# Three attention sweeps on one core: weights turned two steps behind their score, and one run of projection matmuls per step

## The chip, the cores and the metric

The kernel runs on 1 core of one Trainium2 chip. The metric is the device time of one execution in microseconds (us); the median of three runs stands below. Engines are named as the profile names them: PE (TensorE matmuls), PEld (its weight loads), DVE (VectorE), ACT (ScalarE), POOL (GpSimd), SP (SyncE, which issues DMAs).

## What is computed

Three layers on 512 tokens of width 1024, in fp32. Cut to the parts that matter here:

```
def mla_mixer(c_q, c_kv, k_r, pos, ...):                   # layer 1, 12 heads of 64 + 32 rotary
    q  = (rms_norm(c_q, q_norm) @ w_q_up).reshape(B, S, MLA_HEADS, MLA_QK)
    kv = (rms_norm(c_kv, kv_norm) @ w_kv_up).reshape(B, S, MLA_HEADS, MLA_NOPE + MLA_V)
    return causal_block_attention(qf, kf, v, MLA_QK ** -0.5)
def fox_mixer(q, k, v, f_logit, b_f):                      # layer 2, 12 heads of 64
    return causal_block_attention(qh, kh, vh, FOX_DIM ** -0.5, log_f_cum)
def memory_attention(q, k, v):                             # in layers 1 and 2, 4 heads, 256 memory rows
    s = einsum('bshd,bmhd->bhsm', q, k) * MEM_DIM ** -0.5
    return einsum('bhsm,bmhd->bshd', softmax(s), v)
def stick_breaking(q, k, v):                               # layer 3, 16 heads of 64
    log_fail = where(mask, log_sigmoid(-logits), 0)
    between  = cumsum(log_fail, reverse) - log_fail
    w        = where(mask, exp(log_sigmoid(logits) + between), 0);  out = w @ v
```

Every layer is h + rms_norm((attention * silu(gate)) @ w_out) with projections of the normed h ahead of it; the third also has a scan branch.

## The kernel before

The engines' programs are written out by hand, in order, with semaphores between them. A projection in fp32 is three fp32r matmuls for each block: the activations' high part with the weights' high part, high with low, low with high. A weight piece of 1024 columns (512 KB) comes by SP's DMA, ACT writes its high part (`high_part`, L510), POOL the rest (`rest`, L515).

Each attention is a *sweep* over pairs of heads, four steps a pair. A step s is one block of 128 queries for both heads of a pair; its two items are 2s and 2s + 1. The blocks of a causal pair come in the order 3, 0, 2, 1, with 512, 128, 384 and 256 keys. Both layer 1 and layer 2 have 32 steps: two memory pairs (steps 0 to 7, 256 keys) and six causal pairs (8 to 31). Layer 3 has eight causal pairs, also 32 steps. The work of a step:

- PE `score(s)`: L836 (L1910 in layer 3), in layer 1 also L840 for the rotary part, and the mask by a bf16 matmul at L843 (L1913), into banks 2 to 5.
- DVE `lowest` (L933, in layer 2 L929), ACT `exp` (L896), DVE `share` (L939, L942): the weights, in one of four buffers. In layer 3 ACT takes two sigmoids per item (L1984, L1988) and DVE a scan (L2036) and a product (L2042).
- PE `turn_w(i)` (L854, L1925) transposes an item's weights into bank 6 or 7; ACT `collect_w(i)` (L907, L1998) copies them out. `turn_w(i)` waits until item i - 2 is copied out.
- once a pair, PE `values(p)` (L868, L1937) into bank 1, and DVE `weigh` (L950) multiplies by the gate.
- between these, PE projects the next pairs' queries and keys into bank 0: `turn_in(n)` issues the next n matmuls (L1182, L1371, L1894). ACT's `collect(q)` (L1250, L1395, L1971) copies a finished projection q out of bank 0, and `split_ahead_act` then makes the high part of piece q + 2. The first matmul of projection q + 1 waits for that copy. When none is left, `turn_in` issues a filler (`keep_busy`, L668).

In layer 1 two more things stand in the first eight steps: eight units of the values' projection (`v_unit`, L1199; two of them ahead of the sweep, one in each of the steps of `V_STEPS`), whose results ACT or DVE copies out (L1271, L1286), and four transposes of rotary parts (`turn_rope`, L1168) that DVE copies out (L1290). The first causal score waits for all of them.

PE's steps are cut by `counts(s)`, two numbers, matmuls before and after the transposes. The loop before is

```
for s in range(steps + 2):
    score(s)
    before, after = counts(s)
    turn_in(before)
    if beside: beside(s)
    if s % 4 == 1: values(s // 4 - 1)
    turn_w(2 * s - 2); turn_w(2 * s - 1)
    turn_in(after)
```

Each step therefore turns the weights of step s - 1. ACT's loop is exp of step s, `between(s)`, collect_w of step s - 1, `after(s)`; DVE's is lowest, share, weigh, `after(s)`.

Of the kernel before, what the change touches and what calls it, by code (L numbers as in the profile page):

```python
# [30 lines left out]
MB = T // P  # L31
# [188 lines left out]
def build(nc, i, out):  # L220
    ctx = ExitStack()
    with ctx:
# [597 lines left out]
        def sweep_pe(pe, A, turn_in, counts, beside=None):  # L820
# [37 lines left out]
            def values(p):  # L858
                if not 0 <= p < len(A.pairs):
                    return  # L860
                X = A.pairs[p]
                pe.wait_ge(*A.weights_in(8 * p + 8))
                if p:
# [20 lines left out]
        def sweep_act(act, A, between, after):  # L884
# [26 lines left out]
            for s in range(steps + 1):  # L911
# [3 lines left out]
                collect_w(2 * s - 2)  # L915
                collect_w(2 * s - 1)
                after(s)

        def sweep_dve(dve, A, after):
# [33 lines left out]
            for s in range(steps):  # L953
# [4 lines left out]
                if s % 4 == 1:  # L958
                    weigh(s // 4 - 1)
# [186 lines left out]
        V_STEPS = (0, 1, 2, 3, 4, 6)  # L1146
# [7 lines left out]
        def mla_pe(pe):  # L1154
# [32 lines left out]
            def v_unit(u):  # L1187
# [6 lines left out]
                if u == 7:  # L1194
                    pe.wait_ge(*attA.gated(1))
# [30 lines left out]
            def counts(s):  # L1226
                if s < 4:
                    return ((5, 0), (4, 0), (3, 0), (3, 0))[s]
                if s < 4 * MP:
                    return 1, 0  # L1230
# [8 lines left out]
            sweep_pe(pe, attA, turn_in, counts, beside)  # L1239

        def mla_act(act):
# [11 lines left out]
            def after(s):  # L1253
# [7 lines left out]
                if s > last:  # L1261
# [12 lines left out]
            sweep_act(act, attA, between, after)  # L1274
# [3 lines left out]
        def mla_dve(dve):  # L1278
# [17 lines left out]
            sweep_dve(dve, attA, after)  # L1296
# [53 lines left out]
        def fox_pe(pe):  # L1350
# [26 lines left out]
            def counts(s):  # L1377
                if s < 4 * MP:
                    return 6, 0
                if s < 4 * (MP + B_H // 2 - 1):  # L1380
                    return ((8, 6), (8, 2), (10, 6), (8, 0))[s % 4]
                if s < 4 * (MP + B_H // 2):
                    return 3, 3
                return (0, 4) if s % 4 == 0 else (4, 0)
            sweep_pe(pe, attB, turn_in, counts)

        def fox_act(act):
# [10 lines left out]
            def piece(s):  # L1398
                if s < 4 * MP:
                    return s // 4  # L1400
                return 2 * (s // 4 - MP) + 2 + (s % 4 == 3)

            def between(s):
                if s % 4 == 3 and s < 4 * (MP + B_H // 2 - 1):
                    collect(piece(s))

            def after(s):
                if s % 4 == 1 and 4 * MP <= s < 4 * (MP + B_H // 2 - 1):
                    collect(piece(s))
                    split_ahead_act(act, S, 0, piece(s))  # L1410
                if s % 4 == 3 and s < 4 * (MP + B_H // 2 - 1):
                    split_ahead_act(act, S, 0, piece(s))
                if s == 4 * (MP + B_H // 2 - 1):
                    act.wait_ge(C["product"].sem, S.done_after(0, S.n - 1, 0))
                if s > 4 * (MP + B_H // 2 - 1):
                    gated_high(act, attB, s - 4 * (MP + B_H // 2 - 1) - 1)
            sweep_act(act, attB, between, after)
# [3 lines left out]
        def fox_dve(dve):  # L1421
# [5 lines left out]
            sweep_dve(dve, attB, after)  # L1427
# [451 lines left out]
        def stick_pe(pe):  # L1879
# [62 lines left out]
            turn_in(48 + 4)  # L1942
            for s in range(STEPS + 1):
                score(s)
                before, after = ((8, 6), (8, 2), (10, 6), (8, 0))[s % 4]
                before -= 4 * (s == 0)
                if s >= STEPS - 4:
                    before, after = ((6, 6), (6, 6), (6, 6), (6, 0), (6, 0))[s - STEPS + 4]
                turn_in(before)
                if s % 4 == 1:  # L1950
                    values(s // 4 - 1)
                turn_w(2 * s - 2)
                turn_w(2 * s - 1)
                turn_in(after)
# [3 lines left out]
        def stick_act(act):  # L1958
# [47 lines left out]
            for s in range(STEPS + 1):  # L2006
# [3 lines left out]
                if s % 4 == 3 and s < STEPS - 1 or s == STEPS:  # L2010
                    collect(2 * PAIRS + 1 if s == STEPS else 2 * p + 3)
                collect_w(2 * s - 2)
                collect_w(2 * s - 1)
                if s % 4 == 1:
                    collect(2 * p + 2)
                    split(2 * p + 2)
                if s % 4 == 3 and s < STEPS - 1 or s == STEPS:
                    split(2 * PAIRS + 1 if s == STEPS else 2 * p + 3)

        def stick_dve(dve):  # L2020
# [11 lines left out]
            for i in range(2 * STEPS):  # L2032
# [11 lines left out]
                if i % 8 == 2:  # L2044
# [360 lines left out]
```

## Time and profile before

| what | value |
|---|---|
| device time, median of 3 runs | 1221.72 us (1221.5 to 1224.92) |
| the profiled execution's own time | 1220.76 us |
| its span, first to last instruction | 1219.0 us |
| PE busy | 1195.6 us (98%) |
| DVE, ACT, POOL busy | 535.0, 592.5, 429.7 us |
| PE clock granted | 0.999 of full speed |

The span is the time that the trace shows; 1.8 us of the execution's own time lie around it. PE's matmuls are pipelined: a matmul's duration in the trace (0.39 us for 512 columns) is longer than the distance to the next one's start (0.23 us), so what a sequence costs is read from starts, not from durations.

### The profile page before, as it was taken

How to read it: one execution, taken by the hardware profiler on the slowest of the kernel's cores; microseconds unless marked ns; L12 is line 12 of the kernel's file. 1: busy time of each engine (PE TensorE's matmuls, PEld its weight loads, DVE VectorE, ACT ScalarE, POOL GpSimd, SP SyncE). 2: the span in 40 equal slices, each digit the busy share in tenths (PEclk: the TensorE clock that was granted, in tenths of full speed). 3: DMA queues.
4: the chain of work that ended last, by engine and by line, in shares of the span. 5: the costliest groups of instructions: out<-in, count | busy, mean ns of one | idle time of the engine just before them, and what ended most of it. 6: DMA issues, size and time to landing. Idle time of an engine off the chain costs nothing. (4 is left out here: it accounts for less than half of the span.)

```text
span 1219.0 us, 16491 instructions
## 1 busy us (share of the span) xinstructions
PE 1195.6 (98%) x6261; PEld 931.1 (76%) x6261; DVE 535.0 (44%) x978; ACT 592.5 (49%) x1246; POOL 429.7 (35%) x259
## 2 busy tenths in 40 slices
PE   8999999999999999999999999999999999999998
PEld 8988855578988666678888987787666667878886
DVE  4311465643310555452566745601767660033333
ACT  6444655645442655554644654534655552333142
POOL 6534711204344222215344333343322223434451
PEclk9999999999999999999999999999999999999999
DMA  8433211103335999713232321233111113323231
GB/s 310 122 104 67 64 22 44 55 23 95 89 107 81 89 66 73 109 52 89 75 99 56 119 63 59 83 90 104 53 52 52 53 53 91 99 88 103 89 102 69
DMA packets 111407, 100.99 MB, mean 83 GB/s; under 512 B 21141, under 2 KB 98273, under 8 KB 111329
## 3 DMA queue, kind: packets, MB, share of 16 engines
q1 hardware_dynamic: 108784, 95.35, 33.5%
q0 software_dynamic: 864, 3.15, 0.7%
q10 hardware_dynamic: 1680, 1.44, 0.4%
q8 instruction: 50, 0.82, 0.3%
q14 instruction: 29, 0.23, 0.1%
HBM read 94.68 MB, written 2.10 MB: 79 GB/s over the span
## 5 line engine op out<-in xcount | busy, mean ns | idle before, releaser
L515 POOL TENSOR_TENSOR w_lo<-w_raw,w_hi 128x1024 fp32r<-128x1024 f32 (+6 forms) x161 | 362.5, 2252 | 718.6 <-ACT w_hi L510 718.6
L510 ACT ACTIVATE w_hi<-w_raw 128x1024 fp32r<-128x1024 f32 (+6 forms) x161 | 159.9, 994 | 236.1 <-PE bank L570 212.3
L570 PE MATMUL bank<-acts_hi,w_hi 128*128 128x512 f32 (+1 forms) x576 | 224.7, 390 | 3.2 <-DVE acts_lo L2057 1.6
L570 PE MATMUL bank<-acts_lo,w_hi 128*128 128x512 f32 (+1 forms) x576 | 222.9, 387 | 0.0
L570 PE MATMUL bank<-acts_hi,w_lo 128*128 128x512 f32 (+1 forms) x576 | 222.8, 387 | 0.0
L570 PEld LDWEIGHTS bank<-acts_hi,w_hi 128*128 128x128 f32 x576 | 108.3, 188 | 27.9 <-issue 3.8
L570 PEld LDWEIGHTS bank<-acts_lo,w_hi 128*128 128x128 f32 x576 | 108.2, 188 | 22.0
L570 PEld LDWEIGHTS bank<-acts_hi,w_lo 128*128 128x128 f32 x576 | 108.3, 188 | 21.2
L2036 DVE TENSOR_TENSOR_SCAN arena_end<-arena 128x512 f32<-128x512 f32 (+3 forms) x64 | 80.8, 1262 | 63.2 <-ACT arena L1984 63.2
L570 PE MATMUL bank<-w_hi,acts_hi 128*128 128x512 f32 (+4 forms) x248 | 90.0, 363 | 1.6 <-DVE arena L950 1.6
L570 PE MATMUL bank<-w_hi,acts_lo 128*128 128x512 f32 (+4 forms) x248 | 89.4, 361 | 0.0
L570 PE MATMUL bank<-w_lo,acts_hi 128*128 128x512 f32 (+4 forms) x248 | 89.2, 360 | 0.0
L570 PE MATMUL bank<-w_more,acts_hi 128*128 128x512 f32 (+3 forms) x296 | 75.4, 341 | 0.0
L942 DVE TENSOR_SCALAR arena<-arena,stat 128x256 f32<-128x256 f32 (+3 forms) x128 | 65.7, 513 | 4.5
L933 DVE TENSOR_REDUCE stat<-bank 128x1 f32<-128x256 f32 (+3 forms) x80 | 33.4, 458 | 74.3 <-PE bank L836 47.7
L907 ACT ACTIVATE arena<-bank 128x256 f32<-128x256 f32 (+3 forms) x128 | 47.0, 422 | 36.3 <-PE bank L854 36.2
L896 ACT ACTIVATE arena<-bank,stat 128x256 f32<-128x256 f32 (+3 forms) x80 | 39.8, 504 | 39.3 <-DVE stat L933 39.3
L515 POOL TENSOR_TENSOR w_more<-w_raw,w_more 128x1024 fp32r<-128x1024 f32 (+4 forms) x21 | 43.5, 2085 | 43.5 <-ACT w_more L510 43.4
L1894 PE MATMUL bank<-acts_hi,w_hi 128*128 128x512 f32 x144 | 58.6, 407 | 0.0
L1894 PE MATMUL bank<-acts_hi,w_lo 128*128 128x512 f32 x144 | 58.5, 406 | 0.0
L1894 PE MATMUL bank<-acts_lo,w_hi 128*128 128x512 f32 x144 | 57.7, 401 | 0.0
L570 PEld LDWEIGHTS bank<-w_more,acts_hi 128*128 128x128 f32 x296 | 51.6, 189 | 3.8
(293 smaller groups left out, 2142.3 us busy)
## 6 DMA issues: line engine op xcount, KB each, us to landing
w_raw<-in_w_in SPq DMA_DIRECT2D x64, 512.0 KB, 3.6
w_raw<-in_w_out SPq DMA_DIRECT2D x24, 512.0 KB, 3.5
w_raw<-in_w_in_b SPq DMA_DIRECT2D x22, 512.0 KB, 5.3
w_raw<-in_w_in_a SPq DMA_DIRECT2D x10, 512.0 KB, 3.9
w_raw<-in_w_mem_kv SPq DMA_DIRECT2D x8, 512.0 KB, 8.5
w_raw<-in_w_sb_proj SPq DMA_DIRECT2D x8, 512.0 KB, 3.4
w_raw<-in_w_ssd_proj SPq DMA_DIRECT2D x8, 512.0 KB, 3.5
arena_shared<-junk SPq DMA_DIRECT2D x11, 256.0 KB, 20.7
```

The source lines that it names most:

```text
L510: nc.scalar.activation(w_at(p)[0][:, 0:size], w_raw[p % RAW][:, 0:size], ACT.Copy).then_inc(w_high.sem, 1)
L515: nc.gpsimd.tensor_tensor(lo[:, 0:size], w_raw[p % RAW][:, 0:size], hi[:, 0:size].bitcast(F32), ALU.subtract).then_inc(w_rest.sem, 1)
L570: mm = nc.tensor.matmul(bank_of(S, s, g)[0:lhs.shape[1], 0:rhs.shape[1]], lhs, rhs, start=j + kk + t == 0, stop=j == len(S.pieces) - 1 and ...
L896: nc.scalar.activation(w2[i % 4][:, 0:n], src[:, 0:n], ACT.Exp, bias=stat[:, i % 8:i % 8 + 1], scale=-1.0 if X.less else 1.0, accum_out=st ...
L907: nc.scalar.activation(wT2[e][:, 0:blocks, b * P:(b + 1) * P], bank[6 + i % 2][:, 0:blocks * P].rearrange("p (c t) -> p c t", c=blocks), A ...
L933: nc.vector.tensor_reduce(stat[:, i % 8:i % 8 + 1], bank[2 + i % 4][:, 0:n], AX.X, ALU.max, negate=True).then_inc(A.lowest.sem, 1)
L942: nc.vector.tensor_scalar(w2[i % 4][:, 0:n], w2[i % 4][:, 0:n], stat[:, 16 + i % 8:17 + i % 8], None, ALU.mult).then_inc(A.weights.sem, 1)
L1894: mm = nc.tensor.matmul(qk_bank(q)[:, :], w[:, kk * P:(kk + 1) * P], acts[:, kk, :], start=x == 0, stop=x == 23)
L2036: nc.vector.tensor_tensor_scan(left[i % 2][:, T - n:T][:, ::-1], x, x, 1.0, ALU.mult, ALU.bypass).then_inc(sem["scan"], 1)
```

## The change

- In all three sweeps the transposes stand two steps behind: step s turns items 2s - 4 and 2s - 3, and ACT collects them in its step s. The values of a pair come at s % 4 = 2, ahead of the transposes, and `weigh` follows.
- The two runs of projection matmuls of a step are one, at its end. What a step takes is a new table, such that a projection ends with step 0 or 2 of a pair, and ACT collects it there, after `collect_w`.
- The sweep of layers 1 and 2 takes three closing steps where it took two, with 26 fillers in all where there were 32.
- In layer 1 `v_unit` stands ahead of the projections of its step, its last unit in step 5 (was 6), and `values(0)` waits for the copy of it.

```diff
-            for s in range(steps + 2):
+            for s in range(steps + 3) if lag == 2 else ():
+                score(s)
+                if s % 4 == 2:
+                    values(s // 4 - 1)
+                turn_w(2 * s - 4)
+                turn_w(2 * s - 3)
+                if beside:
+                    beside(s)
+                turn_in(counts(s))
...
-                collect_w(2 * s - 2)
-                collect_w(2 * s - 1)
+                collect_w(2 * s - 2 * lag)
+                collect_w(2 * s - 2 * lag + 1)
...
-                if s % 4 == 1:
+                if s % 4 == lag:
                     weigh(s // 4 - 1)
...
-        V_STEPS = (0, 1, 2, 3, 4, 6)
+        V_STEPS = (0, 1, 2, 3, 4, 5)
...
-                    return ((5, 4), (0, 3), (3, 0), (0, 0))[s % 4]
+                    return (QN, 0, KN, 0)[s % 4]
                 if s < 4 * (MP + A_H // 2):
-                    return 3, 3
-                return (0, 4) if s % 4 == 0 else (4, 0)
+                    return 6 * (s % 4 < 3)
+                return 4 * (s % 4 < 2)
...
-                if s < 4 * (MP + B_H // 2 - 1):
-                    return ((8, 6), (8, 2), (10, 6), (8, 0))[s % 4]
+                    return (8, 8, 8, 8, 8, 8, 5, 5)[s]
+                if s < 4 * (MP + B_H // 2 - 1) - 1:
+                    return (14, 10, 14, 10)[s % 4]
...
-            turn_in(48 + 4)
-            for s in range(STEPS + 1):
+            turn_in(48 + 10)
+            for s in range(STEPS + 2):
                 score(s)
...
+                if s > STEPS - 4:
+                    turn_in(6 * (s <= STEPS))
+                else:
+                    turn_in((14, 10, 14, 10)[s % 4])
```

QN is 9 and KN is 6. `last` in ACT's new `after(s)` of layer 2 is step 28; `ended_at` names the steps after which a projection is collected: 2, 5, 8, 10, 12 and so on to 26.

**PE, layer 2, a causal pair.** From the projection matmuls that end step 0 to those of step 1; `waits` names semaphores. Before:

```order
L1371 MATMUL bank<-acts_hi,w_lo 128x512
L836 MATMUL bank<-arena 128x128 [waits lowest]
L836 MATMUL bank<-arena 128x128
L843 MATMUL bank<-later_keys,ident_b 128x128 x2
L1371 MATMUL bank<-acts_lo,w_hi 128x512
```

and now, where the last matmul of the run is also the last of a projection:

```order
L836 MATMUL bank<-arena 128x256
L843 MATMUL bank<-later_keys,ident_b 128x128 x2
L854 MATMUL bank<-ident,arena 128x128 [waits weights_in,weights] x2
L1380 MATMUL bank<-acts_hi,w_hi 128x512 [waits qk_in,w_rest]
L1380 MATMUL bank<-acts_hi,w_lo 128x512
```

The mask's matmul was followed by a projection run; now the transposes follow it and the run comes after them, so the run ahead of the transposes is gone. The second piece is a step 3 with two transposes, then the first matmul of a projection with its wait for the copy out of bank 0.

**PE, layer 1, steps 1 and 2.** `v_unit` is L1199 before, L1208 after; the projection run L1182 before, L1193 after. Before:

```order
L836 MATMUL bank<-arena_end 128x256 x2
L1182 MATMUL bank<-acts_lo,w_hi 128x512
L1182 MATMUL bank<-acts_hi,w_hi 128x512
L1182 MATMUL bank<-acts_hi,w_lo 128x512
L1182 MATMUL bank<-acts_lo,w_hi 128x512
L1199 MATMUL bank<-w_more,acts_hi 128x384 [waits evac]
```

and now:

```order
L836 MATMUL bank<-arena_end 128x256 x2
L1208 MATMUL bank<-w_more,acts_hi 128x384 [waits evac]
L1208 MATMUL bank<-w_more,acts_hi 128x384
L1208 MATMUL bank<-w_more,acts_lo 128x384
L1208 MATMUL bank<-w_more,acts_hi 128x384 x2
L1208 MATMUL bank<-w_more,acts_lo 128x384
L1193 MATMUL bank<-acts_lo,w_hi 128x512
```

The unit's wait for the copy of the unit before it (`evac`) moved ahead of the projection run.

**PE, layer 2, from the last score (step 31) to the last values.** Before:

```order
L836 MATMUL bank<-arena 128x256
L843 MATMUL bank<-later_keys,ident_b 128x128 x2
L668 MATMUL bank<-tri_le,ident 128x128 x3
L854 MATMUL bank<-ident,arena 128x128 [waits weights_in,weights]
L854 MATMUL bank<-ident,arena 128x128 x2
L854 MATMUL bank<-ident,arena 128x128 [waits weights_in,weights]
L854 MATMUL bank<-ident,arena 128x128 x2
L668 MATMUL bank<-tri_le,ident 128x128 x3
```

and now:

```order
L843 MATMUL bank<-later_keys,ident_b 128x128 x2
L854 MATMUL bank<-ident,arena 128x128 [waits weights_in,weights] x3
L854 MATMUL bank<-ident,arena 128x128 x2
L854 MATMUL bank<-ident,arena 128x128 [waits weights_in,weights]
L854 MATMUL bank<-ident,arena 128x128 x2
L668 MATMUL bank<-tri_le,ident 128x128 x4
L854 MATMUL bank<-ident,arena 128x128 [waits weights_in,weights]
L854 MATMUL bank<-ident,arena 128x128
```

Step 31 has no filler now, and step 32's transposes stand right behind step 31's.

## Rows read from the trace of the kernel before

**Rows 1.** The page: span, and PE's busy time.

```profile
span 1219.0 us, 16491 instructions
PE 1195.6 (98%) x6261; PEld 931.1 (76%) x6261; DVE 535.0 (44%) x978; ACT 592.5 (49%) x1246; POOL 429.7 (35%) x259
```

**Rows 2.** Windows: us, busy PE, PEld, DVE, ACT, POOL (instructions), clock, DMA.

```profile
139.05:165.17 26.12, 23.30 (x136) 16.52 (x136) 19.85 (x57) 16.77 (x54) 16.81 (x28) 1.00 0.15 33
165.17:253.88 88.71, 88.59 (x543) 50.89 (x543) 50.45 (x142) 50.68 (x156) 11.60 (x10) 1.00 0.15 44
400.44:423.58 23.14, 22.89 (x116) 14.68 (x116) 15.71 (x49) 16.03 (x50) 4.75 (x2) 1.00 0.93 72
423.58:514.11 90.53, 90.40 (x488) 60.02 (x488) 46.94 (x149) 47.63 (x127) 21.66 (x9) 1.00 0.94 94
514.11:533.81 19.70, 19.67 (x130) 14.00 (x129) 11.53 (x38) 12.32 (x33) 7.10 (x11) 1.00 0.25 81
533.81:543.13 9.32, 7.86 (x62) 5.75 (x61) 4.59 (x16) 6.25 (x19) 0.00 (x0) 1.00 0.01 2
843.44:1000.57 157.13, 156.00 (x846) 104.74 (x845) 113.16 (x135) 91.36 (x223) 38.42 (x16) 1.00 0.20 56
```

**Rows 3.** Waits of PE, layers 2 and 3: us in total, times, longest.

```profile
PE bank L854 <- ACT arena L907: 0.7, 1, 0.7
PE bank L1925 <- DVE arena L2042: 0.8, 2, 0.4
```

**Rows 4.** Timeline of PE, layer 2, end of a pair: start us, us, instruction.

```profile
479.01 0.40 PE L1371 MATMUL bank<-acts_hi,w_hi 128*128 128x512 f32 x1
479.34 0.70 PE L836 MATMUL bank<-arena 64*128 64x256 f32 x4
479.97 0.29 PE L843 MATMUL bank<-later_keys,ident_b 128*128 128x128 bf16 x2
480.07 0.47 PE L1371 MATMUL bank<-acts_hi,w_lo 128*128 128x512 f32 x1
480.38 0.39 PE L1371 MATMUL bank<-acts_lo,w_hi 128*128 128x512 f32 x1
480.61 0.40 PE L1371 MATMUL bank<-acts_hi,w_hi 128*128 128x512 f32 x1
...
481.77 0.39 PE L1371 MATMUL bank<-acts_lo,w_hi 128*128 128x512 f32 x1
482.00 0.82 PE L854 MATMUL bank<-ident,arena 128*128 128x128 f32 x6
482.85 1.13 PE L836 MATMUL bank<-arena 64*128 64x512 f32 x4
```

**Rows 5.** Timeline of PE, layer 1: a mask with the transposes right behind it.

```profile
178.87 0.29 PE L843 MATMUL bank<-later_keys,ident_b 128*128 128x128 bf16 x2
179.00 0.83 PE L854 MATMUL bank<-ident,arena 128*128 128x128 f32 x6
```

**Rows 6.** Timeline of ACT, layer 2: a projection is copied out of bank 0.

```profile
482.20 0.60 ACT L1395 ACTIVATE arena<-bank 128x512 f32<-128x512 f32 x1 [0.34 <-PE bank L1371]
```

**Rows 7.** Timeline of DVE and PE, layer 1, memory pairs.

```profile
143.07 0.54 DVE L1286 COPY hn<-bank 128x384 f32<-128x384 f32 x1
...
156.26 1.94 PE L868 MATMUL bank<-arena,arena_end 128*64 128x512 f32 x8
...
158.24 0.69 DVE L950 TENSOR_TENSOR arena<-bank,arena 128x512 f32<-128x512 f32 x1 [0.39 <-PE bank L868]
...
164.39 0.68 DVE L1290 TENSOR_SCALAR arena<-bank 128x512 f32<-128x512 f32 x1
```

**Rows 8.** Timeline of ACT, POOL and DVE, layer 2, steps 27 and 28.

```profile
523.25 1.07 ACT L510 ACTIVATE w_hi<-w_raw 128x1024 fp32r<-128x1024 f32 x1
...
524.39 2.37 POOL L515 TENSOR_TENSOR w_lo<-w_raw,w_hi 128x1024 fp32r<-128x1024 f32 x1 [6.08 <-ACT w_hi L510]
...
525.83 1.21 DVE L942 TENSOR_SCALAR arena<-arena,stat 128x512 f32<-128x512 f32 x1
...
527.15 0.49 DVE L942 TENSOR_SCALAR arena<-arena,stat 128x512 f32<-128x512 f32 x1
```

**Rows 9.** Timeline of ACT and PE, layer 2, behind the last score (533.81).

```profile
536.35 0.49 ACT L896 ACTIVATE arena<-arena,stat 128x256 f32<-128x256 f32 x1
...
537.45 0.80 PE L854 MATMUL bank<-ident,arena 128*128 128x128 f32 x4 [0.67 <-ACT arena L907]
...
539.96 2.37 PE L868 MATMUL bank<-arena 128*64 128x512 f32 x16
```

More of the change, by code:

```diff
@@ L862, in values @@
                 pe.wait_ge(*A.weights_in(8 * p + 8))
+                if bank_free and p == 0:
+                    pe.wait_ge(*bank_free)
                 if p:
@@ L870, in values @@
                 mm.then_inc(A.valued.sem, 1)
-            for s in range(steps + 2):
+            for s in range(steps + 3) if lag == 2 else ():
[7 more added lines that the diff above has]
+                turn_in(counts(s))
+            for s in range(steps + 2) if lag == 1 else ():
                 score(s)
@@ L882, in sweep_pe, with sweep_act @@
                 turn_in(after)
-        def sweep_act(act, A, between, after):
+        def sweep_act(act, A, between, after, lag=1):
             steps = len(A.steps)
@@ L909, in collect_w @@
                                      ACT.Copy).then_inc(A.weights_in.sem, 1)
-            for s in range(steps + 1):
+            for s in range(steps + lag):
                 exp(2 * s)
@@ L914, in sweep_act, with sweep_dve @@
                 between(s)
-                collect_w(2 * s - 2)
-                collect_w(2 * s - 1)
+                collect_w(2 * s - 2 * lag)
+                collect_w(2 * s - 2 * lag + 1)
                 after(s)
-        def sweep_dve(dve, A, after):
+        def sweep_dve(dve, A, after, lag=1):
             steps = len(A.steps)
@@ L1238, in mla_pe @@
             pe.wait_ge(*pA_qr.evac(MB))
-            sweep_pe(pe, attA, turn_in, counts, beside)
+            sweep_pe(pe, attA, turn_in, counts, beside, lag=2, bank_free=pA_v.evac(2 * MB))
         def mla_act(act):
@@ L1260, in after @@
                     split_ahead_act(act, S, 0, q)
-                if s > last:
+                if last < s <= last + 4:
                     gated_high(act, attA, s - last - 1)
@@ L1273, in mla_act @@
             keep_v(1)
-            sweep_act(act, attA, between, after)
+            sweep_act(act, attA, between, after, lag=2)
             for c in range(4, len(attA.pairs)):
@@ L1295, in after @@
                     gated_low(dve, attA, s - last - 2)
-            sweep_dve(dve, attA, after)
+            sweep_dve(dve, attA, after, lag=2)
             for c in range(2, len(attA.pairs)):
@@ L1396, in collect @@
                                      scale=(HD ** -0.5, 1.0)[q % 2]).then_inc(qk_in.sem, 1)
[L1398 to L1405, printed above, removed]
-            def after(s):
[L1408 to L1413, printed above, removed]
+            ended_at = {2: 0, 5: 1}
+            ended_at.update((4 * MP + 2 * n, 2 + n) for n in range(S.n - 2))
+            last = 4 * (MP + B_H // 2 - 1)
+            def after(s):
+                if s in ended_at:
+                    collect(ended_at[s])
+                    split_ahead_act(act, S, 0, ended_at[s])
+                if s == last:
                     act.wait_ge(C["product"].sem, S.done_after(0, S.n - 1, 0))
-                if s > 4 * (MP + B_H // 2 - 1):
-                    gated_high(act, attB, s - 4 * (MP + B_H // 2 - 1) - 1)
-            sweep_act(act, attB, between, after)
+                if last < s <= last + 4:
+                    gated_high(act, attB, s - last - 1)
+            sweep_act(act, attB, lambda s: None, after, lag=2)
             for c in range(4, len(attB.pairs)):
@@ L1426, in after @@
                     gated_low(dve, attB, s - 4 * (MP + B_H // 2 - 1) - 2)
-            sweep_dve(dve, attB, after)
+            sweep_dve(dve, attB, after, lag=2)
             for c in range(2, len(attB.pairs)):
@@ L1940, in values @@
                 mm.then_inc(sem["s_out"], 1)
-            turn_in(48 + 4)
-            for s in range(STEPS + 1):
+            turn_in(48 + 10)
+            for s in range(STEPS + 2):
                 score(s)
[L1945 to L1950, printed above, removed]
-                    values(s // 4 - 1)
-                turn_w(2 * s - 2)
-                turn_w(2 * s - 1)
-                turn_in(after)
+                if s % 4 == 2:
+                    values(s // 4 - 1)
+                turn_w(2 * s - 4)
+                turn_w(2 * s - 3)
+                if s > STEPS - 4:
+                    turn_in(6 * (s <= STEPS))
+                else:
+                    turn_in((14, 10, 14, 10)[s % 4])
             pe.wait_ge(sem["sig"], 4 * STEPS)
@@ L2005, in stick_act @@
             split(1)
-            for s in range(STEPS + 1):
+            for s in range(STEPS + 2):
                 p = s // 4
@@ L2009, in stick_act @@
                 chances(2 * s + 1)
[L2010 to L2018, printed above, removed]
+                collect_w(2 * s - 4)
+                collect_w(2 * s - 3)
+                if s % 2 == 0 and s < STEPS - 2 or s == STEPS:
+                    q = 2 * PAIRS + 1 if s == STEPS else 2 * p + 2 + s % 4 // 2
+                    collect(q)
+                    split(q)
         def stick_dve(dve):
```

17 lines of the change are left out of this document (7 added, 10 removed).

## The prediction

> **What bounds the kernel now.** I read the page first: PE is busy for 1195.6 of 1219.0 us [rows 1], so only what PE issues, or waits for, can change the time. Next the windows over the three sweeps, cut at the score of step 0, of step 8, of the last pair and of step 31 [rows 2]. The causal steps of layers 1 and 2 leave PE almost nothing idle: 90.40 busy of 90.53 us in layer 2's, 88.59 of 88.71 in layer 1's. The gaps are at the ends: the memory steps of layer 1 (23.30 of 26.12) and the 9.32 us behind layer 2's last score (7.86). Then PE's waits: 0.7 us for one `collect_w` at the end of layer 2, 0.8 in two places for the stick-breaking weights, once at the start and once at the end of layer 3 [rows 3]. Last the timeline of one pair, where the distance between starts shows what an order costs [rows 4, 5].
>
> **What the merged runs save.** In the middle of a projection run the next matmul starts 0.23 us after the last (480.38 to 480.61). The first of a run takes 0.31 (480.07 to 480.38) [rows 4]. Ahead of it the mask's two matmuls take 0.10 (479.97 to 480.07); with transposes behind them they take 0.13 (178.87 to 179.00) [rows 4, 5]. So each run that started behind a mask cost 0.08 - 0.03 = 0.05 us more than it will when it joins the run that starts behind the transposes. The other borders (run to score, transposes to run, values) stay as many as they were. Layer 1 loses two such run starts a pair, x5 = 0.5 us. Layer 2 loses four a pair (0.05 each, 0.19 with roundings), x5 = 0.95, and six in the memory steps, where no mask stands ahead and I take 0.1 each with the two borders of `values(0)`: 0.8. Layer 3: 7 pairs x 0.19, and a little at the ends, 1.4.
>
> A second gain is a wait. At the end of a pair the projection's last matmul starts at 481.77 [rows 4]; ACT's copy of it runs from 482.20 to 482.80 [rows 6] and the next pair's score starts at 482.85 [rows 4]. The transposes ahead of it (six from 482.00, 0.11 apart) would have let it start at 482.75. The keys are now ready one step earlier, so 0.1 us goes, in 5 pairs of layer 2 and 7 of layer 3, and 0.2 more at layer 2's step 8: 0.7 and 0.7. Layer 3's two waits of 0.4 for the weights (0.8 [rows 3], some 1.1 counted between starts) go too, as the weights have a whole step more.
>
> **What the change costs.** *Layer 1's start, +0.7.* `v_unit(3)` waits until DVE has copied unit 2 out, which ends at 143.61 [rows 7]. Before, four projection matmuls covered this; now it follows the score of step 1, whose 0.63 us end at some 142.8 by my count, and PE stands for 1.0 us. That alone would be made good by step 5. But the first causal score waits for DVE's last rotary copy (ends 165.07 [rows 7], score 165.17 [rows 2]), and that chain gets longer: in step 6 the two exps need the transposes that now stand behind `values(0)` (1.94 us [rows 7]), and DVE does `weigh` (0.69) and a rotary copy (0.68) [rows 7] after them, ahead of the maxima of step 7. Laying the steps out one by one with these durations I get 165.9 for the score.
>
> *Layers 1 and 2, last pair.* `turn_w(i)` needs item i - 2 copied out, and ACT copies that only after the exps of the step before. With a run of ten matmuls in step 3 of a pair this is hidden. Step 27 has no run left. In layer 2 ACT then goes from the projection's copy (1.1 us after its last matmul's start) to the high part of the next piece (1.07 [rows 8]), to two exps and to the copy: the transposes of step 28 stand some 0.65 us.
>
> Worse, POOL starts its 2.37 us on that piece right behind the high part. In the trace a `share` that starts meanwhile (525.83) takes 1.21 us instead of 0.49 and ends just after POOL does [rows 8]. After the change the shares of step 27, two instead of one, fall into POOL's time; DVE reaches the maxima of step 28 at 2.2 us later than the score allows, and step 29's transposes, which need a copy behind the exps of step 28, stand 1.75 us. So layer 2 pays 2.4. In layer 1 the score is longer (L840), which covers the first and most of the second: 0.3.
>
> *Behind the last score, +0.25 each in layers 1 and 2.* Before, the last transposes start at 537.45, 3.64 us behind the score at 533.81, and the values at 539.96 [rows 9]. Now step 32's transposes stand first: they need the copy of step 29's weights, which ACT does after the last exp (starts 536.35 [rows 9]), so about 3.4 us behind the score; then 6 transposes (0.65), four fillers (0.9), 4 transposes (0.45), four fillers (0.9): values at 6.4 instead of 6.15. That six fillers fewer are issued therefore gives nothing back.
>
> *Smaller.* The lag leaves two transposes fewer ahead of layer 2's last score (-0.2, they stand in the tail) and two more in layer 1's causal window (+0.2). Layer 3: the fourth projection starts at step 1 with no transposes ahead and waits 0.3 for the copy of the third; `turn_w(60)` 0.25. The DMAs are the same and so is their order; SP is ahead by four pieces and POOL's piece is needed 3 us or more after it ends: nothing.
>
> **Sum.** Layer 1: +0.7 - 0.5 + 0.2 + 0.3 + 0.25 = +0.9. Layer 2: -0.95 - 0.8 - 0.7 - 0.2 + 2.4 + 0.25 = 0.0. Layer 3: -1.4 - 0.7 - 1.1 + 0.55 = -2.7. Together -1.8 us: the profiled execution's 1220.76 becomes 1219.0. The median stands 0.96 above that execution, so I predict 1219.9. The unknown terms are layer 1's start (0 to 1.2) and layer 2's last pair (0 to 3, by whether the shares meet POOL's instruction and for how long).
>
> **A rule that speaks against the gain.** The trace shows 0.31 for the first matmul of a run, although the mask, the transposes and the projections all use the whole array (128*128 [rows 4]). The Trainium skill (TensorEngine Tiling (Array Packing), "Key Properties") says that changing the tiling mode drains TensorE. By that rule alone only scores (64*128) and values (128*64) would cost a change, the change has just as many of these, and the 3.65 us of the run starts would not be there: the sum would be -1.8 + 3.65 = +1.85, 1223.6. I go by the row.
>
> **The rivals.**
> 1. *All of it is hidden* (0.18). ACT and DVE keep up in the last pairs and layer 1's start is as long as before. For it: they are busy less than half the time [rows 1]. Against: the ends of the sweeps are where PE waits today. Without the waits that I add (0.7, 0.3, 2.4, 0.55, 0.5) it is -6.2 us: 1215.5; without the meeting with POOL alone (1.75 + 0.3) -3.9: 1217.8.
> 2. *Bank 0 comes free too late* (0.07), slower. A projection now ends a step, and the next starts behind one score and two or four transposes: 0.33 to the score, 0.63 for it, 0.13 for the mask, 0.11 for the transposes [rows 4, 5], 1.2 us after the last matmul's start. The copy ends 1.03 after it [rows 6], up to 1.1 where ACT has another wait ahead of it, and PE sees it 0.05 later. So 0.05 us is what is left, at some 25 places of layers 2 and 3. If ACT is still at `collect_w` (moved ahead of the copy) or at a delayed exp when the projection ends, each place costs the delay: 0.3 us each would be +7.5, 1225.7 after everything else. It decides from about 0.2 us each. Against: by the durations ACT is free 1 us or more ahead.
> 3. *Run starts cost the same wherever they stand* (0.05), so that 3.65 us of the gain is not there: the cost sits in the change of the kind of matmul and not in a run's start, 1223.6, within 0.3%.
>
> **How the numbers follow.** A measurement of this kernel can tell about 0.3%, 3.7 us, from no change. My forecast has 0.70: 1219.9, with bounds of its own of 1217.8 to 1222.5 by the two unknown terms; 0.02 of it lies below -3.7. Faster by over 0.3%: that and rival 1, 0.20. Slower: rival 2 less the 0.01 where its delay is small, 0.06. The same: the rest with rival 3, 0.74. The range leaves out the best end of rival 1 and most of rival 2: 1216.6 to 1223.2.
>
> **What would show it.** In the changed profile a causal pair of layer 2 should take 19.6 us from score to score (19.9 before), one of layer 1 14.9 (15.0), one of layer 3 19.6. The first matmul of a run should still take 0.31. Layer 1's step 8 score should start 26.8 us behind its first (26.1 before), with PE idle about 1 us ahead of `v_unit(3)`. Layer 2's steps 28 and 29 should show waits of PE at the transposes, for `collect_w`, of 0.6 and 1.7 us, and a `share` of step 27 of some 1.5 to 2 us. The wait ahead of step 32's transposes should be 1.5 us or more. No wait for the stick-breaking product should be left. I am wrong if the pairs' time does not fall, if waits for `collect(q)` stand ahead of the first matmuls of projections, or if the last pairs show none.

## The result, and the profile after

The changed kernel takes 1224.67 us (median of 21 executions, 1223.28 to 1226.30), the kernel before 1221.69 (21 executions); the ratio is 1.0017, its 95% interval [1.0011, 1.0024], all of it above 1. I predicted 1219.9, a range of 1216.6 to 1223.2, and most likely no difference that can be told. The difference is indeed under 0.3%, but it is on the other side, 3.0 us slower instead of 1.8 faster, and above the range. The profiled execution is the longest of the 21, 1226.30 us, 5.5 above the one of before. The traces explain these 5.5; for the median, 1.6 below that execution, they are a guide.

The page of the changed kernel, its span, PE's busy time and the line of PE's granted clock. In the clock's line each digit is a slice of 30.6 us; the 8 is the slice from 153 us:

```profile
span 1224.6 us, 16443 instructions
PE 1192.8 (97%) x6237; PEld 931.0 (76%) x6237; DVE 541.6 (44%) x978; ACT 590.5 (48%) x1246; POOL 431.3 (35%) x259
PEclk9999989999999999999999999999999999999999
```

PE is busy 2.8 us less than in [rows 1] and the span is 5.6 longer: it waits more. The windows of the same places as in [rows 2] (us, busy PE, PEld, DVE, ACT, POOL, clock, DMA):

```profile
139.74:166.49 26.75, 22.85 (x133) 15.76 (x132) 20.04 (x57) 16.14 (x52) 16.76 (x28) 1.00 0.15 31
166.49:174.55 8.06, 8.06 (x23) 4.16 (x23) 2.57 (x6) 2.00 (x6) 0.00 (x0) 0.58 0.00 0
406.57:430.79 24.22, 24.22 (x122) 15.51 (x122) 15.06 (x47) 15.99 (x49) 7.15 (x3) 1.00 0.93 81
430.79:516.82 86.03, 85.92 (x469) 58.55 (x468) 50.06 (x147) 44.42 (x122) 19.05 (x8) 1.00 0.95 84
516.82:541.55 24.73, 20.71 (x141) 13.79 (x140) 14.01 (x45) 13.29 (x39) 6.92 (x11) 1.00 0.31 103
541.55:552.68 11.13, 8.16 (x51) 6.19 (x51) 4.56 (x14) 6.88 (x19) 0.00 (x0) 0.85 0.01 1
854.39:1006.12 151.73, 151.59 (x840) 103.61 (x839) 115.21 (x135) 89.43 (x222) 39.62 (x16) 1.00 0.20 56
```

The second row is layer 1's step 8, 8.06 us at a mean granted clock of 0.58, where every window of [rows 2] has 1.00. The one before last is layer 2's tail at 0.85, 11.13 us instead of 9.32. Layer 1's tail reads the same:

```profile
258.08:269.26 11.18, 8.79 (x55) 6.48 (x54) 4.52 (x12) 6.73 (x19) 0.00 (x0) 0.85 0.00 0
```

against 9.27 before. So in three stretches of 6.8, 3.4 and 3.4 us, starting at 166.6, 262.2 and 545.5, the granted clock is at its lower level of 1.2 GHz. (Both traces have one more in their last 4 us, where PE runs nothing.) How PE comes to the first, and below it to the second, in its timeline:

```profile
162.44 0.68 PE L854 MATMUL bank<-ident,arena 128*128 128x128 f32 x4 [0.25 <-ACT arena L918]
163.87 0.66 PE L1179 MATMUL bank<-ident,arena 128*128 128x128 f32 x4 [0.74 <-DVE arena L1299]
166.49 1.98 PE L836 MATMUL bank<-arena 64*128 64x512 f32 x4 [1.96 <-issue]
168.39 2.08 PE L840 MATMUL bank<-arena 32*128 32x512 f32 x4
...
261.46 0.84 PE L854 MATMUL bank<-ident,arena 128*128 128x128 f32 x6 [1.60 <-ACT arena L918]
```

PE had been idle for 0.25, 0.74 and 1.96 us within 4.3 us; then the score takes 1.90 us to the start of its rotary part (1.06 at full clock, in e2 below). The kernel before also stands there, 0.17 us and then 1.79 in one piece, and its score runs at full clock, 1.06 us to the rotary part:

```profile
165.17 1.13 PE L836 MATMUL bank<-arena 64*128 64x512 f32 x4 [1.79 <-issue]
```

So what is new ahead of step 8 is above all more waits in a row; the long one grew by 0.17. Layer 2's tail:

```profile
544.88 0.92 PE L854 MATMUL bank<-ident,arena 128*128 128x128 f32 x6 [2.18 <-ACT arena L918]
545.60 1.92 PE L668 MATMUL bank<-tri_le,ident 128*128 128x128 f32 x8
547.30 1.06 PE L854 MATMUL bank<-ident,arena 128*128 128x128 f32 x4
```

Four fillers (eight matmuls in the trace) take 1.70 us from start to start, against 0.9 at full clock (e1 below). The third new thing is in layer 2's step 26. PE, and ACT in step 24:

```profile
517.67 0.29 PE L843 MATMUL bank<-later_keys,ident_b 128*128 128x128 bf16 x2
519.86 2.37 PE L870 MATMUL bank<-arena 128*64 128x512 f32 x16 [1.90 <-ACT arena L918]
```

```profile
513.54 0.60 ACT L1404 ACTIVATE arena<-bank 128x512 f32<-128x512 f32 x1 [0.83 <-PE bank L1380]
517.45 1.06 ACT L510 ACTIVATE w_hi<-w_raw 128x1024 fp32r<-128x1024 f32 x1 [3.30 <-DMA w_raw<-in_w_out]
```

ACT stood 3.30 us for the DMA of a piece of the output weights, with the exps of step 25 (from 518.41) and the copies that the values need queued behind it.

Where the 5.5 us between the two profiled executions come from, by place (score starts; the low clock's share is the place's time less the same place at full clock in the runs below):

| place | predicted | measured |
|---|---|---|
| ahead of layer 1's first score (nothing changed there) | 0 | +0.7 |
| layer 1, step 0 to 8 | +0.7 | 26.75 - 26.12 = +0.6 |
| layer 1, step 8 to 31 | 0.0 | +2.9, of it low clock +3.2 |
| layer 1, tail | +0.25 | 11.18 - 9.27 = +1.9, of it low clock +1.65 |
| layer 2, step 0 to 31 | -0.25 | 134.98 - 133.37 = +1.6, of it DMA wait 1.9 |
| layer 2, tail | +0.25 | 11.13 - 9.32 = +1.8, of it low clock +1.6 |
| layer 3, from its first projection matmul | -2.7 | -4.0 |

### The profile page after: what moved, and what is told of

Read it like the earlier page. It is cut to its first block, busy times and chain, and to the rows that moved or that the text cites. A ratio compares the mean times of both kernels' runs of the same rounds, so it can differ in the third digit from the quotient of the medians.

```text
span 1224.6 us, 16443 instructions
## 1 busy us (share of the span) xinstructions
PE 1192.8 (97%) x6237; PEld 931.0 (76%) x6237; DVE 541.6 (44%) x978; ACT 590.5 (48%) x1246; POOL 431.3 (35%) x259
## 4 chain that ended last, share of the span: by engine, by line
PE 87%; DMA 5%; ACT 3%; DVE 2%; issue 1%; POOL 1%; SPq 0%; ACTq 0%; DVEq 0%
PE bank L570 47%; PE bank L1896 8%; PE bank L1589 6%; PE bank L1380 3%; PE bank L836 3%; PE bank L854 3%; PE bank L870 3%; PE bank L1912 2%; DMA w_raw<-in_w_out 2%; DMA w_raw<-in_w_in_b 2%; PE bank L1193 2%; PE bank L1927 2%; PE bank L1939 2%; DMA w_raw<-in_w_mem_kv 1%; PE bank L840 1%
## 5 line engine op out<-in xcount | busy, mean ns | idle before, releaser
L2033 DVE TENSOR_TENSOR_SCAN arena_end<-arena 128x512 f32<-128x512 f32 (+3 forms) x64 | 83.9, 1310 | 60.3 <-ACT arena L1984 60.3
L953 DVE TENSOR_SCALAR arena<-arena,stat 128x256 f32<-128x256 f32 (+3 forms) x128 | 71.2, 557 | 4.5
L854 PE MATMUL bank<-ident,arena 128*128 128x128 f32 x304 | 47.2, 284 | 6.6 <-ACT arena L918 6.6
```

The lines of the kernel that those rows point to most:

```text
L854: mm = nc.tensor.transpose(bank[6 + i % 2][:, c * P:(c + 1) * P], w2[i % 4][:, c * P:(c + 1) * P], ident[:, :])
L953: nc.vector.tensor_scalar(w2[i % 4][:, 0:n], w2[i % 4][:, 0:n], stat[:, 16 + i % 8:17 + i % 8], None, ALU.mult).then_inc(A.weights.sem, 1)
L2033: nc.vector.tensor_tensor_scan(left[i % 2][:, T - n:T][:, ::-1], x, x, 1.0, ALU.mult, ALU.bypass).then_inc(sem["scan"], 1)
```

## The experiments

The theory after reading the traces: the change shortens the pairs as predicted; it lost because new idle time of PE lets the clock fall to 1.2 GHz in layer 1's step 8 and in two tails, and because the earlier high part waits for its DMA. The rivals: the places are long for other reasons and the clock is beside the point; run starts cost nothing; ACT is overloaded. The kernel before, measured again beside each group of runs, had medians of 1221.64 to 1221.69. The runs are called e1 to e12.

**Fillers in the tails (e1).** In both layers' `counts`:

```diff
-                    return 6 * (s % 4 < 3)
+                    return (6, 6, 6, 8)[s % 4]
```

> The changed kernel with 8 filler matmuls in step 31 of layers 1 and 2, where it has none; they stand in the time in which PE waits for step 32's transposes (1.60 and 2.18 us in the changed kernel's trace). Theory clock: PE's idle time there lets the granted clock fall to the 1.2 GHz level, and the transposes and fillers behind it cost double; from the last score to the last values should be 6.3 us in both layers instead of 8.0, the clock of these stretches 1.0, and the kernel about 3 us faster than the changed one: 1221.5. Rival chain: the last values are late by ACT's and DVE's chain of the last weights, whatever PE does meanwhile; the stretch stays at 8.0 us and the time at 1224.7.

1221.48 us, ratio to before 0.9993 [0.9983, 1.0003]. Both tails at full clock; layer 1's, score to values:

```profile
256.40 0.70 PE L836 MATMUL bank<-arena 64*128 64x256 f32 x4
...
258.02 1.95 PE L668 MATMUL bank<-tri_le,ident 128*128 128x128 f32 x16
259.81 0.83 PE L854 MATMUL bank<-ident,arena 128*128 128x128 f32 x6
260.47 1.06 PE L668 MATMUL bank<-tri_le,ident 128*128 128x128 f32 x8
261.36 0.60 PE L854 MATMUL bank<-ident,arena 128*128 128x128 f32 x4
262.79 2.37 PE L870 MATMUL bank<-arena,arena_shared 128*64 128x512 f32 x16
```

The values start 6.39 us behind the score, where the changed kernel takes 8.02. The edit adds 24 fillers: 8 in each tail and, as `counts` of layer 2 uses this line from step 27 on, 8 in layer 2's step 27, where they take the place of waits (steps 27 to 31 take 15.15 us with and without them). This work that nobody reads makes the kernel 3.2 us faster: the clock theory, and not a chain of ACT and DVE. Layer 1's step 8 is at 1.2 GHz in this trace too, for 3.4 us instead of 6.8 (6.42 us instead of 8.06), so some of the profiled executions' difference is how long a low stretch lasts.

**Fillers in layer 1's step 7 (e2).**

```diff
+                if s == 4 * MP - 1:
+                    pe.wait_ge(*attA.gated(1))
+                    keep_busy(pe, 3, 1)
...
                         turn_rope(x - QKN)
+                        if x == QKN + RG:
+                            keep_busy(pe, 8, 1)
```

> The changed kernel with fillers in layer 1's step 7: 3 ahead of the last rotary transposes (wait of 1.0 us there) and 8 behind them (2.0 us). Theory clock: the step 8 score, its rotary part and the projection run behind it took 3.15 us more than before only since the clock was at 1.2 GHz after the idle time; step 8 to 9 should take 4.9 us instead of 8.06, and the kernel 1221.5, 3.1 less than the changed one. The chain of DVE that delays the score of step 8 by 0.6 us stays. Rival contention: the 8.06 us come from something else in that place (the DMAs, or a wait for bank 0) and stay: 1224.7.

1219.26 us, 0.9971 [0.9960, 0.9983]: 5.4 less than the changed kernel, more than the 3.1 expected. Step 8 of it:

```profile
164.64 1.95 PE L668 MATMUL bank<-tri_le,ident 128*128 128x128 f32 x16
166.65 1.13 PE L836 MATMUL bank<-arena 64*128 64x512 f32 x4
167.71 1.13 PE L840 MATMUL bank<-arena 32*128 32x512 f32 x4
```

The window of step 8 is 4.87 us:

```profile
166.65:171.52 4.87, 4.87 (x23) 2.68 (x24) 2.11 (x6) 1.70 (x6) 0.00 (x0) 1.00 0.00 0
```

The score comes as late as before the edit, 26.75 us behind the first: that delay costs 0.6 and is another matter (e12); the other 3.2 were the clock. The surprise is the rest: both tails are at full clock too, although they have the same waits as in the changed kernel (1.6 and 2.2 us). The idle time makes the fall possible, it does not bring it each time.

**Layer 1 as before (e3).** `mla_pe`, `mla_act`, `mla_dve` and `V_STEPS` of the kernel before, the rest as changed.

> Layer 1's sweep as in the kernel before, layers 2 and 3 as changed. Theory clock plus the terms read from the two traces: layer 1 costs +0.64 (start) +2.88 (step 8 at half clock less the merged runs) +1.91 (tail) = 5.4 us in the profiled executions; without it the kernel should be at about 1219.5, 2 below the kernel before, and its trace should show only one stretch at 1.2 GHz, behind layer 2's last score. If the low clock in the profiled execution is rare in the other executions, the gain is the 0.9 us of start and tail alone: 1223.8.

1219.53 us, 0.9980 [0.9968, 0.9991], as the clock theory said and far from the 1223.8 of its rival. One low stretch, in layer 2's tail:

```profile
536.02:547.20 11.18, 8.21 (x52) 6.14 (x51) 4.64 (x14) 6.94 (x19) 0.00 (x0) 0.85 0.01 1
```

**Layer 3 alone (e4).** `stick_pe`, `stick_act` and `stick_dve` as changed, the rest as before.

> Only layer 3's sweep as changed, layers 1 and 2 as before. By the prediction's terms -2.7 us (1219.0); by the two traces -4.05 us (1217.6): the window from its first projection matmul to the end of the sweep. No stretch of the trace should be at 1.2 GHz behind the first layer's start. If the run starts had cost nothing (rival 3 of the prediction), -1.3: 1220.4.

1217.56 us, 0.9964 [0.9954, 0.9975]: -4.1, the traces' term and not the prediction's. Here the third part of the change beats the kernel before by itself.

**Two runs of projection matmuls a step, lag kept (e8)** (on the kernel of the last experiment):

```diff
                 score(s)
+                ahead = (6, 0, 6, 0)[s % 4] if 0 < s <= STEPS - 4 else 0
+                turn_in(ahead)
...
-                    turn_in((14, 10, 14, 10)[s % 4])
+                    turn_in((14, 10, 14, 10)[s % 4] - ahead)
```

> As e4_l3_alone (layer 3 as changed, the others as before), but in steps 0 and 2 of a pair of layer 3 six of the 14 projection matmuls stand ahead of the transposes, behind the mask: two more run starts a pair, the lag and everything else as in e4. Theory of the prediction: 0.05 us each, a pair 19.6 instead of 19.50, the kernel 0.7 to 0.8 slower than e4: 1218.3. Rival 3 (run starts cost the same wherever they stand, the gain comes from the lag alone): pairs at 19.50, 1217.6.

1218.41 us, 0.9968 [0.9957, 0.9979], 0.85 above e4. A causal pair of e4, then of this kernel:

```profile
862.05:881.54 19.49, 19.49 (x109) 13.30 (x108) 14.14 (x17) 11.30 (x28) 4.78 (x3) 1.00 0.19 55
```

```profile
864.20:883.87 19.67, 19.67 (x110) 13.20 (x109) 14.11 (x17) 11.31 (x28) 4.76 (x3) 1.00 0.20 53
```

A run start behind the mask costs 0.09 us (0.18 for two), more than the 0.05 predicted. From the first score of layer 3 to the last the two traces differ by 1.25 us, the medians by 0.85. Rival 3 of the prediction falls. This trace also has a low stretch of 3.4 us in layer 1's step 8, where its program is that of the kernel before:

```profile
166.47:172.95 6.48, 6.48 (x24) 3.77 (x24) 2.57 (x6) 2.12 (x6) 0.00 (x0) 0.74 0.00 0
168.40:171.80 3.40, 3.40 (x12) 2.48 (x11) 2.31 (x6) 1.45 (x4) 0.00 (x0) 0.50 0.00 0
```

**The high part behind layer 2's projection 10 one step later (e5).** It is the high part of the first piece of the output weights (`in_w_out` in the rows above), made when projection 10 is copied out.

```diff
                     collect(ended_at[s])
-                    split_ahead_act(act, S, 0, ended_at[s])
+                    if s < last - 4:
+                        split_ahead_act(act, S, 0, ended_at[s])
+                if s == last - 3:
+                    split_ahead_act(act, S, 0, S.n - 2)
+                if s == last - 2:
+                    split_ahead_act(act, S, 0, S.n - 1)
```

> The changed kernel, but in layer 2 ACT makes the high part of the last but one piece at the end of step 25 instead of step 24, where in the changed kernel's trace it waits 3.30 us for that piece's DMA with the exps of step 25 queued behind it. Theory DMA: PE's 1.90 us ahead of the values in step 26 is this wait passed on; it should be gone, step 26 to 27 take 7.6 us instead of 9.57 and the kernel 2 us less, 1222.7. Rival: values in step 26 wait for ACT's copies because ACT has too much in its steps 24 and 25; the wait stays at 1 us or more and the time at 1224. The waits of steps 28 and 29 stay (0.5 and about 1.5).

1222.24 us, 0.9999 [0.9990, 1.0009], 2.4 less than the changed kernel. PE's values in step 26, 0.22 us behind the mask's last start (517.48), and ACT in step 25:

```profile
517.70 2.38 PE L870 MATMUL bank<-arena 128*64 128x512 f32 x16
```

```profile
517.35 1.06 ACT L510 ACTIVATE w_hi<-w_raw 128x1024 fp32r<-128x1024 f32 x1 [1.60 <-DMA w_raw<-in_w_out]
```

ACT still waits for the DMA, but with nothing behind it that PE needs; steps 26 to 27 take 7.58 us instead of 9.57. ACT was not overloaded. The wait at this place differs from trace to trace: 1.9 us in the changed kernel, 1.4 in e1 and e3, 1.0 in e10 and e12, 0.6 in e2.

**The high part behind projection 11 in step 32 as well (e6)** (`s == last - 2` becomes `s == last + 4`).

> As e5_late_split, and the high part of the last piece made in step 32 instead of step 26, so that POOL's 2.35 us on it meet no share. Theory of the prediction: the 1.86 us share of step 27 falls to 0.35, and PE's waits in steps 28 and 29 (0.65 and 1.75 predicted) go: 2.4 us less than e5, 1220.3. Rival: those waits come from the exps' place in ACT's order alone, POOL meets them by chance: the waits stay within 0.3 us and the time within 0.5 of e5.

1222.12 us, 1.0001 [0.9989, 1.0012]. The share of step 27 in the changed kernel, and POOL beside it:

```profile
528.12 2.35 POOL L515 TENSOR_TENSOR w_lo<-w_raw,w_hi 128x1024 fp32r<-128x1024 f32 x1 [7.19 <-ACT w_hi L510]
```

```profile
528.76 1.86 DVE L953 TENSOR_SCALAR arena<-arena,stat 128x256 f32<-128x256 f32 x1
```

and here:

```profile
525.37 0.35 DVE L953 TENSOR_SCALAR arena<-arena,stat 128x256 f32<-128x256 f32 x1
```

Steps 29 to 30 take 2.90 us instead of 4.38, 28 to 29 3.87 instead of 3.97. That is 1.6 us, not the 2.4 expected of this edit; 0.4 to 0.5 us of wait stays at step 28. The edit takes ACT's high part out of step 26 together with POOL's instruction and so doesn't part the two. The rows do: in the changed kernel ACT stood idle for DVE ahead of the exps of step 28, so it was the long share that held PE up and not ACT's own work:

```profile
531.73 0.72 ACT L907 ACTIVATE arena<-arena,stat 128x512 f32<-128x512 f32 x1 [2.38 <-DVE stat L940]
```

The median is only 0.1 below e5, which is the number that the rival gave. The profiled trace has three low stretches, of 3.4 us each (layer 1's step 8 and both tails). The mean clock of the ten executions is 0.9938 here and 0.9950 in e5; by my estimate that is 1.5 us (0.0012 of 1222), about what the edit gained.

**The parts put together (e7, e9).** e7: layer 1 as before, both high parts late, the fillers of e1 in layer 2.

> Layer 1's sweep as before; layer 2's as changed with both high parts late as in e6_late_both and 8 fillers in step 31 as in e1_tail_fillers; layer 3's as changed. By the terms read so far against the kernel before: layer 3 -4.05, layer 2's sweep +1.4 - 2.1 - 2.4 = -3.1, its tail +0.2: -6.9, 1214.8. If the DMA of layer 2 sets its pace (20.8 us a pair against PE's 19.5) the wait only moves on to the next user of a piece, and layer 2 gives -1: 1216.8.

1217.67 us, 0.9972 [0.9962, 0.9982]: above both numbers, and not for the rival's reason. The line of e1 also puts 8 fillers into step 27, where PE has no wait: 27 to 28 takes 2.86 us instead of 1.08. Put right (e9):

```diff
-                    return (6, 6, 6, 8)[s % 4]
+                    return 8 if s == 4 * (MP + B_H // 2) - 1 else 6 * (s % 4 < 3)
```

> As e7_best, but the 8 fillers of layer 2 stand in step 31 alone: in e7 the same line had put 8 into step 27 too, where 27 to 28 took 2.86 us instead of 1.08 and PE had no such wait (S(27) to S(31) 14.82 us against e6's 13.57). Theory: 1.2 us less than e7, 1216.4, and 5.3 less than the kernel before. If fillers in step 27 only take the place of waits there, as they did in e1 (15.15 us with and without them), nothing changes: 1217.7.

1216.46 us, 0.9959 [0.9945, 0.9973]. Its PE waits in layer 2's last pair and tail:

```profile
PE bank L570 <- DVE arena L961: 0.8, 1, 0.8
PE bank L854 <- ACT arena L918: 0.8, 2, 0.4
PE bank L870 <- ACT arena L918: 0.4, 1, 0.4
```

where the changed kernel has

```profile
PE bank L854 <- ACT arena L918: 4.3, 3, 2.2
PE bank L870 <- ACT arena L918: 1.9, 1, 1.9
```

No long wait moved on to a later step, as the rival for e7 had it, though its number (1216.8) is near. Against the first number, 1214.8, the meeting with POOL was worth 1.6 us and not 2.4, and the tail of layer 2 takes 9.98 us instead of e2's 9.49, with the high part now in it.

**The changed kernel with every long idle stretch filled (e10)** (e2's edit, and step 31's fillers in both layers), **then with both high parts late (e11).**

> The changed kernel with fillers in every long idle stretch: 3 and 8 in layer 1's step 7 (e2), 8 in step 31 of layers 1 and 2. Theory clock: no stretch at 1.2 GHz in the trace, and no execution with one: the runs, which in e2 lay between 1216.8 and 1220.8, come closer together, median 1218.5 to 1219.3; what is left against the kernel before is the change without the clock's part (-1.8 predicted). Rival: e2's 5.4 us gain on the changed kernel had another source than the clock and these fillers at the tails only add work: 1219.5 or more, spread as e2's.

1217.82 us, 0.9972 [0.9962, 0.9982], eight executions from 1217.54 to 1219.46, no low stretch in the trace. This is the change with its clock held by 27 fillers: 3.8 us faster than the kernel before, and below the 1218.5 to 1219.3 expected. The mean clock of its executions is 0.998 to 1.000, where all 21 of the changed kernel have 0.993 to 0.996.

> As e10_fill_all with layer 2's two high parts late as in e6_late_both. Theory: 3.2 us less than e10 (the DMA wait 2.0, the shares 1.5, less 0.3 of new waits), 1215.8; against e9 it tells whether layer 1's sweep as changed is worth having once its clock is held: by the traces it costs 0.6 us (sweep +0.3, tail +0.3), so e9 should be no slower. Rival: the clock falls again at layer 2's now earlier places, 1217.5.

1216.28 us, 0.9955 [0.9940, 0.9969], from four executions: 1.5 below e10, not 3.2. In the traces layer 2's sweep is 2.6 us shorter, since the DMA wait had only 1.05 left in e10 (step 26 to 27 took 8.63 there), and the way to layer 3's first score 0.5 longer, as the high part now stands in the tail. It can't be told from e9. Both beat both kernels.

**Where layer 1's start loses its 0.6 us (e12)** (on e2's kernel).

```diff
+                if s < 4:
+                    turn_in(counts(s))
                 if beside:
                     beside(s)
-                turn_in(counts(s))
+                if s >= 4:
+                    turn_in(counts(s))
```

> As e2_fill_step7, but in steps 0 to 3 of layer 1 the unit of the values' projection stands behind the projection matmuls again, as before. Theory of the prediction: PE's wait of 0.9 us ahead of the unit in step 1 goes (step 1 to 2: 3.0 to 3.3 us instead of 3.76), but the step 8 score still starts 26.7 us behind the first, since DVE's chain of weigh and rotary copies sets it. Rival: that wait is where layer 1's start loses its 0.6 us, and the step 8 score comes at 26.1.

1218.72 us, a single execution, so only its trace is used. Step 1 to 2 takes 2.84 us instead of 3.76, and the step 8 score starts 26.64 us behind the first instead of 26.75. So the wait ahead of the unit isn't what delays it. By the rows it is DVE in steps 6 and 7, which no run tried by itself:

```profile
161.57 0.16 DVE L953 RECIPROCAL stat<-stat 128x1 f32<-128x1 f32 x1 [2.13 <-ACT arena L910]
...
162.50 0.68 DVE L964 TENSOR_TENSOR arena<-bank,arena 128x512 f32<-128x512 f32 x1
163.09 0.68 DVE L1307 TENSOR_SCALAR arena<-bank 128x512 f32<-128x512 f32 x1
...
165.66 0.68 DVE L1307 TENSOR_SCALAR arena<-bank 128x512 f32<-128x512 f32 x1
```

**All traces together.** Counted over the 14 traces, each with two tails and one step 8. Tails with fillers in step 31, or with the old order: 17, none with a low stretch. Tails with the wait unfilled: 11 (changed, e2, e5, e6 and e12 two each, e3 one), 6 with one. Step 8 behind the changed start, unfilled: 4 of 4 low (changed, e1, e5, e6); filled: 0 of 4; in the old order: 1 of 6 (e8), behind idle times of 0.2 and 1.8 us.

The kernel before isn't free of it either. Of its 81 executions in the three groups of runs, 14 took 1224.4 to 1225.0 us at a mean clock of 0.996 or 0.997, the others 1220.4 to 1222.9 at 0.997 to 0.999. Where these 14 lose it no trace shows. The changed kernel has no execution at 0.997 or above.

## Why the prediction was wrong

- *The sum has no term for the clock.* This is the step that failed. "What the change costs" priced each new wait of PE (layer 1's start, "behind the last score, +0.25 each") by its own length. It even forecast the wait of 1.5 us or more ahead of step 32's transposes (1.60 and 2.18 measured), and none of its signs of being wrong looked at the clock. It read six fillers fewer as "gives nothing back", and nothing at all as the price of their loss. In the profiled execution, the longest, the low clock cost 3.2 + 1.65 + 1.6 = 6.5 us. Over all 21 the mean clock is 0.994, against 0.999 in e10; I estimate 6.1 us from that (0.005 of 1224), or up to 1.3 less, as the low clock of the idle last microseconds costs nothing. The runs took it back by adding work: -3.2 (e1), -5.4 (e2), -6.9 (e10) against the changed kernel. What is left of the 6.9 was not traced; e10's wait for the DMA is 0.9 us shorter.
- *"The DMAs are the same and so is their order; SP is ahead by four pieces ...: nothing"* was wrong. The order is the same, but projection 10 now ends in step 24 instead of 25, so the high part behind it asks for its piece earlier: 5.8 us behind step 24's score (3.30 ahead of 517.45, against 508.31), where before it began 12.0 behind it (514.76 against 502.76). That was 1.9 us of PE in this trace, moved off by e5.
- *Layer 2's last pair, 2.4 us:* the forecast chain is in the trace. The waits are 0.5 and 1.6 us (0.65 and 1.75 predicted), the share 1.86 (1.5 to 2).
- *The run starts* cost 0.09 us and not 0.05 (e8): pairs of layers 2 and 3 take 19.50 us, where 19.6 was predicted, and layer 1's 14.90. Layer 3 gave -4.0 instead of -2.7. The pairs make some 0.7 of the 1.3 us; the rest lies at its ends and was not taken apart. With its clock held the change gains 3.8 us (e10), where the sum said 1.8.
- *Layer 1's start, +0.7:* measured +0.6. e12 rules out the wait ahead of the unit; the chain of DVE that was named fits the rows.
- *The tails' 6.4 us from score to values* (its terms add up to 6.3): 6.39 in layer 1 and 6.32 in layer 2 at full clock (e1).
- *Rival 1* (all hidden) gave 1217.8 without the meeting with POOL; e10 comes to 1217.82, by a larger gain less waits that are there, so that the numbers agree is luck. *Rival 2:* no wait for `collect(q)` stands ahead of a projection in the changed trace, and layer 3's window is 151.59 busy of 151.73. Its "1225.7 after everything else" doesn't follow: 1219.9 + 7.5 is 1227.4. *Rival 3* fell with e8; its 1223.6 lies above the range's 1223.2, which the text on the range doesn't say.
- Part of the difference between profiled executions is none of the change: 0.7 us ahead of the first score, which 11 of the 12 experiments' traces have too. The one of before is an early one, as is e10's, as its 0.96 below the median hinted.

## What to carry to other kernels

In this kernel a filler or a projection matmul that covered a wait of PE was worth more than its own length. So before taking one away, ask what would follow at half clock, and count fillers as part of the schedule. Compare the mean clock of all executions as well as the times: here it showed in every one of the 21. When work is moved one step ahead, every user of a transfer on that path is moved too: compare the new time of need with the landing, and put what nobody needs soon (the next stage's weights) behind what PE waits for.

## What the runs showed of the hardware

- The granted clock fell from 2.4 to 1.2 GHz in 4 of 4 places where PE had been idle for 0.25, 0.74 and 1.96 us in layer 1's step 7, in 6 of 11 where it had been idle for 1.60 or 2.18 us in one piece in a tail, and in 1 of 6 where it had been idle for 0.2 and 1.8 us ahead of step 8 in the old order. Each of these low stretches lasted 3.4 or 6.8 us. At the lower level the four score matmuls of 512 columns start 0.48 us apart (166.49 to 168.39) instead of 0.27. The Trainium skill (TensorE: Matmul & The Clock Gate, "What's actually happening") says that the gate's ratio takes two values alone, for 1.2 and 2.4 GHz; the trace agrees, 0.50 and 1.00.
- A DVE `tensor_scalar` on fp32 that starts while POOL's two-input instruction runs ends only just behind it, by the trace: it took 1.86 us instead of 0.35 (to 530.62, POOL to 530.47), and 1.89 instead of 0.28 for 128 columns (519.12 to 521.01 in the changed kernel, POOL to 520.93). The Trainium skill (SBUF — State Buffer, "SBUF: two separate sides") calls the port pair that DVE and POOL share an exclusive lock, which the first to start holds for its whole instruction; the trace agrees.
- In layer 2 the DMA engines are busy 0.95 of the causal window and move only 84 GB/s. The lines of the DMA view from 490 to 520 us of the changed kernel, in slices of 0.75 us:

```profile
GB/s 19 35 90 311 332 333 274 131 52 29 33 22 25 33 19 33 27 22 36 22 27 30 16 38 22 25 33 16 35 27 44 126 366 369 399 410 401 380 287 68
...
w_raw<-in_w_out SPq DMA_DIRECT2D x4, 512.0 KB, 13.3
arena_shared<-junk SPq DMA_DIRECT2D x2, 256.0 KB, 18.1
```

For some 16 us the engines move 16 to 38 GB/s, while the two broadcasts of a row to 128 partitions (L1357, 256 KB each, issued at 489.92) are under way; the weight piece issued at 494.69 landed at 517.4, behind them. A group of two pieces and two broadcasts takes 20.5 and 21.8 us (SP's issues at 452.40, 472.89 and 494.69), PE's pair 19.5. In the kernel before the groups take 20.8 and 21.0 us (446.42, 467.17 and 488.12), the pair 19.9. So the shorter pair finds its pieces later. That the broadcasts set this pace is read from these rows; it wasn't tried by a run.
